# Unit 7 of the down projection as seven block products too, with some of the weight sums made by adding DMAs

## The reference

```python
h = rms_norm(x, ffn_norm[i])
u = causal_depthwise_conv(h @ w_up[i], conv_w[i], conv_b[i])
x = x + (jax.nn.silu(u[..., :D_FF]) * u[..., D_FF:]) @ w_down[i]
x = x + (p[i] @ ple_proj[i]) * jax.nn.sigmoid(x @ ple_gate[i])
```

## Time and profile before

| | us |
|---|---|
| median of 3 runs | 658.11 |
| lowest, highest | 657.94, 658.22 |
| profiled execution | 658.76 |
| its span in the trace | 656.9 |
| granted TensorE clock | 1.0 throughout |

### The profile page before, as it was taken

One profiled execution on the slowest core, in us unless ns is written; L12 is line 12 of the kernel. 1 busy time (PEld: TensorE's weight loads), 2 busy tenths in 40 slices (PEclk: granted clock), 3 DMA queues, 4 the chain that ended last, 5 costly groups with the idle time before them and its releaser, 6 DMA issues.

```text
span 656.9 us, 9644 instructions
## 1 busy us (share of the span) xinstructions
PE 648.3 (99%) x3774; PEld 558.8 (85%) x3774; DVE 507.4 (77%) x729; ACT 432.2 (66%) x649; POOL 329.4 (50%) x196
## 2 busy tenths in 40 slices
PE   8999999999999999999999999999999999999997
PEld 6988887888888888888889879878888888888885
DVE  5997778749878768996488777886699778789933
ACT  6669886676766674654474789856776766664632
POOL 5443500288888885006841353004888888820091
PEclk9999999999999999999999999999999999999999
DMA  9972125675555555653387431165555555555411
GB/s 320 372 252 65 65 101 160 198 247 192 189 187 191 185 189 191 212 196 108 109 287 248 154 102 65 66 196 189 193 192 193 191 189 189 188 194 204 161 32 65
DMA packets 74606, 115.38 MB, mean 176 GB/s; under 512 B 2368, under 2 KB 58432, under 8 KB 74304
## 3 DMA queue, kind: packets, MB, share of 16 engines
q1 hardware_dynamic: 73408, 111.95, 51.0%
q10 hardware_dynamic: 1152, 2.81, 1.2%
HBM read 113.70 MB, written 1.05 MB: 175 GB/s over the span
## 4 chain that ended last, share of the span: by engine, by line
PE 94%; DVE 3%; DMA 1%; ACT 1%; issue 0%; POOL 0%; SPq 0%; DVEq 0%; ACTq 0%; POOLq 0%
PE ps L1580 24%; PE ps L1027 14%; PE ps L1029 14%; PE ps L1028 14%; PE ps L1582 12%; PE ps L1173 1%; PE ps L1079 1%; DMA raw<-w_in 1%; PE ps L1199 1%; PE ps L1439 1%; PE ps L1041 1%; PE ps L1114 1%; PE ps L1211 1%; DVE hn L2286 1%; PE ps L1640 1%; PE ps L1642 1%
## 5 line engine op out<-in xcount | busy, mean ns | idle before, releaser
L496 POOL TENSOR_TENSOR wl<-raw,wh 128x2048 fp32r<-128x2048 f32 (+1 forms) x58 | 259.0, 4468 | 155.9 <-DVE x L2275 90.5
L1580 PE MATMUL ps<-hT_hl,wh 128*128 128x512 f32 x688 | 238.6, 392 | 0.0
L627 ACT ACTIVATE wh<-raw 128x2048 fp32r<-128x2048 f32 (+1 forms) x100 | 180.5, 1808 | 49.9 <-DVE raw L2216 23.6
L1582 PE MATMUL ps<-hT_hl,wl 128*128 128x256 f32 x688 | 193.3, 281 | 0.0
L1580 PEld LDWEIGHTS ps<-hT_hl,wh 128*128 128x128 f32 x688 | 129.1, 188 | 28.2
L1582 PEld LDWEIGHTS ps<-hT_hl,wl 128*128 128x128 f32 x688 | 129.4, 188 | 0.0
L1027 PE MATMUL ps<-wh,hT_hl 128*128 128x512 f32 (+1 forms) x216 | 79.7, 369 | 0.0
L1029 PE MATMUL ps<-wh,hT_hl 128*128 128x512 f32 (+1 forms) x216 | 77.4, 358 | 0.0
L1028 PE MATMUL ps<-wl,hT_hl 128*128 128x512 f32 (+1 forms) x216 | 77.4, 358 | 0.0
L483 POOL TENSOR_SCALAR st<-st 128x2 f32<-128x2 f32 (+3 forms) x22 | 6.5, 294 | 114.0 <-ACT lat L702 62.2
L2175 DVE SCALAR_TENSOR_TENSOR pb<-ps,conv,pb 128x255 f32<-128x255 f32 (+1 forms) x96 | 39.5, 472 | 17.3 <-ACT pb L918 17.3
(11 more groups left out here) (362 smaller groups left out, 1281.5 us busy)
## 6 DMA issues: line engine op xcount, KB each, us to landing
raw<-w_up SPq DMA_DIRECT2D x44, 1024.0 KB, 5.1
raw<-w_down SPq DMA_DIRECT2D x22, 1024.0 KB, 4.9
raw<-w_in SPq DMA_DIRECT2D x16, 1024.0 KB, 9.7
raw<-w_o SPq DMA_DIRECT2D x6, 1024.0 KB, 4.9
raw<-ple_gate SPq DMA_DIRECT2D x6, 1024.0 KB, 4.8
raw<-w_in SPq DMA_DIRECT2D x4, 704.0 KB, 5.2
ng<-norm_gains ACTq DMA_DIRECT2D x2, 1024.0 KB, 6.7
raw<-w_o SPq DMA_DIRECT2D x4, 512.0 KB, 4.0
```

The costliest lines, as they stand in the source:

```text
L496: pool.tensor_tensor(wl[:, slot, 0:n], raw[:, slot, 0:n], w_high(u)[:, 0:n].bitcast(F32), ALU.subtract).then_inc(done, 1)
L627: act.activation(w_high(u)[:, c:n], raw[:, slot, c:n], ACT.Copy).then_inc(h_made, 1)
L1580: pe.matmul(both, high[:, c], hU_all[:, k].rearrange("p a n -> p (a n)"), start=k == 0, stop=False, skip_group_check=True)
L1582: mm = pe.matmul(o, wl[:, slot, c], hU_h[:, k, :], start=False, stop=k == KT - 1, skip_group_check=True)
```

## The change

`SEVEN` gets unit 7, so that units 4, 6, 7 and 8 are made of seven products. The place for the sums is laid out anew: `t3` of all four units lies in the upper half of the region of `hT_hl`, t2 and t4 in two alternating places in the lower half.

Two of the four weight sums are now made by DMAs. When PE has finished the last up unit, SP copies the four b12 blocks (256 KB each) from w_down to their `t3` places, before it loads unit 5. POOL waits for all four, then adds b22 to `t3` of the first unit and b11 to b12 in the raw slot of the same unit with a DMA each, both ahead of its low part of down unit 2; those of the other three units are issued behind it, the second kind when the raw unit has landed. DVE adds only t2 and t4. ACT's high part of a seven unit waits for the DMA that makes the sum in the raw slot.

The sums of the activations (`act_sums`, unchanged) move from the down stage to the step of the up stage that follows the product, in the place where `product_low` stands for ordinary steps. `weight_rest` and the high parts of the weight sums become two instructions each.

```diff
@@ -75,7 +75,7 @@
-SEVEN = (4, 6, 8)
+SEVEN = (4, 6, 7, 8)
 FEW = len(SEVEN)
@@ -150,7 +150,8 @@
     "silu": STEPS, "prod": STEPS, "g_high": STEPS - FEW, "g_low": STEPS - FEW,
-    "w_sums": 4 * FEW, "a_sums": FEW, "a_rounded": FEW, "a_rest": FEW, "w_rounded": FEW, "w_rest": FEW,
+    "w_sums": 2 * FEW, "b12_landed": 16 * FEW, 
+    **{f"t{n}_made_{i}": 16 for n in (1, 3) for i in range(FEW)}, "a_sums": FEW, "a_rounded": FEW, "a_rest": FEW, "w_rounded": FEW, "w_rest": FEW,
     "down_low": STEPS - DVE_FROM, "sevens_done": 1, "sevens_copied": 2, "sevens_added": 1,
@@ -215,7 +216,7 @@
         hT = sb("hT", [P, KT, SEQ])
-        with nc.sbuf_tensor("quarters", [P, 2, 1536], F32) as quarters:
+        with nc.sbuf_tensor("quarters", [P, 4096], F32) as quarters:
             pass
@@ -319,9 +320,25 @@
+        def t3_sum(i):
+            return quarters[:, 2048 + i * 512:2048 + (i + 1) * 512]
+        def t3_low(i):
+            return hT_hl[:, 2048 + i * 512:2048 + (i + 1) * 512]
+        def t2_t4(i):
+            return quarters[:, (i % 2) * 1024:(i % 2 + 1) * 1024]
+        def weight_rows(i, k):
+            return slice((2 * SEVEN[i] + k) * P, (2 * SEVEN[i] + k + 1) * P)
...
-            return hT_hl[:, (i % 2) * 1536:(i % 2 + 1) * 1536]
+            return hT_hl[:, (i % 2) * 1024:(i % 2 + 1) * 1024]
@@ -438,6 +455,11 @@
                 for s in range(STEPS):
+                    if s == DEEP - 1:
+                        unit_done(sp, layer, U_DOWN - 1)
+                        for i in range(FEW):
+                            sp.dma_start(t3_sum(i), w_down[layer][weight_rows(i, 0), 0:512]
+                                         ).then_inc(F["b12_landed"], 16)
                     load(rows(w_down, 2 * s, 2), U_DOWN + s)
@@ -590,9 +612,31 @@
                 pool.wait_ge(F["hn_ready"], base["hn_ready"] + 4)
-                for u in (*range(U_POOL, U_DOWN + DVE_FROM), *range(U_GATE, UNITS)):
-                    if u == U_GATE:
-                        pool.wait_ge(F["sevens_added"], base["sevens_added"] + 1)
+                def add_to_t1(i):
+                    u = U_DOWN + SEVEN[i]
+                    slot = u % DEEP
+                    pool.wait_ge(raw_landed[slot],
+                                 (layer * (UNITS // DEEP) + u // DEEP + 1) * 16)
+                    pool.dma_start(raw[:, slot, 0:512], w_down[layer][weight_rows(i, 0), 512:1024],
+                                   accum_op=ALU.add).then_inc(F[f"t1_made_{i}"], 16)
+                def add_to_t3(i):
+                    pool.dma_start(t3_sum(i), w_down[layer][weight_rows(i, 1), 0:512],
+                                   accum_op=ALU.add).then_inc(F[f"t3_made_{i}"], 16)
+                for u in range(U_POOL, U_DOWN + DVE_FROM):
+                    if u == U_DOWN + DVE_FROM - 1:
+                        pool.wait_ge(F["b12_landed"], base["b12_landed"] + 16 * FEW)
+                        add_to_t3(0)
+                        add_to_t1(0)
+                    low(u)
+                for i in range(1, FEW):
+                    add_to_t3(i)
+                    add_to_t1(i)
+                pool.wait_ge(F["sevens_added"], base["sevens_added"] + 1)
+                for u in range(U_GATE, UNITS):
                     low(u)
@@ -944,8 +988,9 @@
                         act.wait_ge(F["g_low"], base["g_low"] + eights(STEPS - 1))
-                    act.wait_ge(F["w_sums"], base["w_sums"] + 4 * i + 4)
-                    act.activation(quarter_highs(i), quarters[:, i % 2], ACT.Copy
+                    act.wait_ge(F["w_sums"], base["w_sums"] + 2 * i + 2)
+                    act.activation(quarter_highs(i)[:, 0:1024], t2_t4(i), ACT.Copy)
+                    act.activation(quarter_highs(i)[:, 1024:1536], t3_sum(i), ACT.Copy
                                    ).then_inc(F["w_rounded"], 1)
@@ -967,7 +1012,7 @@
                     if s in SEVEN:
-                        act.wait_ge(F["w_sums"], base["w_sums"] + 4 * SEVEN.index(s) + 2)
+                        act.wait_ge(F[f"t1_made_{SEVEN.index(s)}"], 16 * (layer + 1))
                     high(U_DOWN + s)
@@ -1616,10 +1661,11 @@
                     product(6, s2, high, low, 0)
-                    mm = product(7, s3, high, low, 1)
+                    mm = split_product(ps[:, 7, :], *s3, high[:, 1024:1536], t3_low(i), i == 0,
+                                       i == FEW - 1)
                     if i == FEW - 1:
                         mm.then_inc(F["sevens_done"], 1)
-                    product(1, a22, high, low, 2).then_inc(w_used, 1)
+                    product(1, a22, high, low, 1).then_inc(w_used, 1)
@@ -2189,34 +2235,6 @@
-                dve.wait_ge(F["conv_landed"], base["conv_landed"] + 16)
-                for s in range(STEPS):
-                    summed(s, 0)
-                    if s and s - 1 not in SEVEN:
-                        product_low(s - 1)
-                    taps(s, 0)
-                    summed(s, 1)
-                    taps(s, 1)
-                    product(s)
-                product_low(STEPS - 1)
-                def weight_sums(i):
-                    u = U_DOWN + SEVEN[i]
-                    slot = u % DEEP
-                    dve.wait_ge(raw_landed[slot],
-                                (layer * (UNITS // DEEP) + u // DEEP + 1) * 16)
-                    unit_done(dve, layer, U_DOWN + SEVEN[i - 2] if i > 1 else U_DOWN - 1)
-                    b12, b11, b22, b21 = (raw[:, slot, n * 512:(n + 1) * 512] for n in range(4))
-                    t2, t3, t4 = (quarters[:, i % 2, n * 512:(n + 1) * 512]
-                                  for n in range(3))
-                    tt(t3, b12, b22, ALU.add).then_inc(F["w_sums"], 1)
-                    for n, (o, one, two) in enumerate(((b12, b12, b11), (t2, b12, b22),
-                                                       (t4, t2, b21))):
-                        tt(o, one, two, ALU.add).then_inc(F["w_sums"], 1)
-                        if n < 2:
-                            dve.wait_ge(F["w_sums"], base["w_sums"] + 4 * i + n + 2)
@@ -2229,6 +2247,32 @@
+                dve.wait_ge(F["conv_landed"], base["conv_landed"] + 16)
+                for s in range(STEPS):
+                    summed(s, 0)
+                    if s and s - 1 not in SEVEN:
+                        product_low(s - 1)
+                    elif s:
+                        act_sums(SEVEN.index(s - 1))
+                    taps(s, 0)
+                    summed(s, 1)
+                    taps(s, 1)
+                    product(s)
+                product_low(STEPS - 1)
+                def weight_sums(i):
+                    u = U_DOWN + SEVEN[i]
+                    slot = u % DEEP
+                    t2, t4 = (t2_t4(i)[:, n * 512:(n + 1) * 512] for n in range(2))
+                    dve.wait_ge(raw_landed[slot],
+                                (layer * (UNITS // DEEP) + u // DEEP + 1) * 16)
+                    unit_done(dve, layer, U_DOWN + SEVEN[i - 2] if i > 1 else U_DOWN - 1)
+                    dve.wait_ge(F[f"t3_made_{i}"], 16 * (layer + 1))
+                    tt(t2, t3_sum(i), raw[:, slot, 512:1024], ALU.add).then_inc(F["w_sums"], 1)
+                    dve.wait_ge(F["w_sums"], base["w_sums"] + 2 * i + 1)
+                    tt(t4, t2, raw[:, slot, 1536:2048], ALU.add).then_inc(F["w_sums"], 1)
@@ -2243,8 +2287,9 @@
                     dve.wait_ge(F["w_rounded"], base["w_rounded"] + i + 1)
-                    o = quarter_sums(i)
-                    tt(o, quarters[:, i % 2], quarter_highs(i).bitcast(F32), ALU.subtract
+                    highs = quarter_highs(i).bitcast(F32)
+                    tt(quarter_sums(i), t2_t4(i), highs[:, 0:1024], ALU.subtract)
+                    tt(t3_low(i), t3_sum(i), highs[:, 1024:1536], ALU.subtract
                        ).then_inc(F["w_rest"], 1)
@@ -2258,7 +2303,7 @@
                         weight_sums(SEVEN.index(s))
-                        act_sums(SEVEN.index(s))
+                        dve.wait_ge(F["w_sums"], base["w_sums"] + 2 * SEVEN.index(s) + 2)
                     down_low(s)
```

## The result

The changed kernel takes 664.35 us (median of 5 runs, 663.67 to 665.21), the kernel before 658.11 (657.89 to 658.28): a ratio of 1.0094, with an interval of 1.0083 to 1.0105. It is slower by 6.2 us. The forecast was 660.3, with a range of 656.6 to 664.0. The sign was right, the size was not: the loss is 4.1 us larger than forecast and ends just outside the range.

What follows compares the result with a forecast made beforehand. TensorE's matmul count plus PE's waits was taken as the bound. Per layer, 1.8 us of waits at units 2 and 8 less 0.68 saved, twice, adds 2.2 to 658.11: 660.3 us, range 656.6 to 664.0.

Steps and rivals of the forecast that it cites:

- The saving: Down stage, PE: unit 7 goes from 24 to 21 matmuls, 0.68 us a layer, 1.36 in all.
- The fourth sum: Up stage, step 9: VectorE's fourth activation sum starts 0.05 us after POOL's recorded start; taken to pass, at no cost.
- The gaps of 0.92, 0.79 and 0.66: Between POOL operations in up steps 5 and 7, 8, and 9; the fourth sum starts 0.71 us after POOL's end.
- a later sum of over 4 us: Sign of being wrong: any activation sum but the first of each four at over 4 us.
- Rival (1): Up step 9: fourth sum misses POOL's gap, waits 4.6 us; 3.5 - 0.68 = 2.8 a layer, 663.7; missed gap 15%.
- The landing at 253.4: Four b12 DMAs, 1024 KB together like one w_down load, start at 248.5 and land 4.9 us later.
- POOL's start of the issues at 253.5: Released by the copies, POOL issues two adding DMAs, starts unit 2's low part at 255.5, ends it at 260.1.
- Two branches, 1.8 each: Last up product held: PE waits 0.9 before unit 2, 0.9 before unit 8; product first: 1.8 before unit 2.
- The price of an issue: POOL's issue of an adding DMA: taken as 1.0 us, with bounds of 0.45 and 1.76.
- VectorE's chain of 26.24: From unit 3's low part to unit 8's activation rests VectorE needs 26.24 us, PE 25.16; a lead of 1.08 is needed.
- Landing of the adding DMAs "costs nothing": Sums by adding DMAs wanted after 263 for unit 4; landing can take 8 us, at no cost.

Runs made afterwards that it cites:

- With the gap mended: Changed kernel with only unit 8's activation sums moved out of step 9, behind the last low part of the up stage: 664.27 us, ratio 1.0090.
- the last kernel: Changed kernel with a semaphore for the first copy, unit 8's activation sums behind the last up low part, and its t2 made early: 657.80 us, ratio 0.9992.
- the kernel with t1 early: Changed kernel, unit 8's sums moved; POOL issues unit 4's t1 before unit 2's low part, waits for copies only behind it: 658.47 us, ratio 0.9998.

## Why the prediction was wrong

- *The saving* of 0.68 a layer, 1.36 in all, was right as far as the runs can tell: 1.07 by the medians, 1.24 by the means.
- *The fourth sum, "costed at nothing".* This is the step that failed first. The gaps of 0.92, 0.79 and 0.66 (measured 0.92, 0.80 and 0.66) and the start 0.05 behind POOL were right in both layers, and the text then set them aside on the ground that some time passes between a recorded start and the first read. The sum that started 0.05 behind was held for 4.72, so not even 0.05 of such time was there; the text had itself named a later sum of over 4 us as a sign of being wrong. Rival (1) describes what came and should have been the forecast: 3.5 of waits a layer (3.3 and 3.1 measured) and 663.7 (664.35 measured). Its parts were less exact than its sum. It has 1.4 before unit 1; measured were 0.94 before unit 0, where PE waits for VectorE's late taps, and 0.20 before unit 1. The half microsecond a layer of slower matmuls behind the gaps, on which the text had nothing, takes the total above 663.7.
- *The landing at 253.4, and POOL's start of the issues at 253.5.* This step failed too, and by itself it would have cost as much. The bytes were those of one load, and SP began to issue when it was expected to (248.47), but the fourth copy released POOL 6.0 later and not 4.9: at 254.3 to 254.6 in both layers of three kernels and one layer of a fourth, at 255.3 in its other layer, 0.8 to 1.8 later than the text has it (all with the last up matmul put at 248.24). With the gap mended the kernel still took 664.27, with 2.08 and 2.64 before unit 2 where the text has 0.9 or 1.8. Why four copies take longer than one load of the same bytes was not tried.
- *Two branches, 1.8 each.* The text had either a held product (0.9 before unit 2, 0.9 before unit 8) or a product that comes first and a late subtraction (1.8 before unit 2, nothing before unit 8). With the gap mended each branch occurs in one layer: the product is held in layer 0 (2.08 and 0.95) and takes 0.69 in layer 1, where its low part is held instead (2.64 and 0.45). They cost the same, as the text had it, but 3.03 and 3.09. The late landing explains most of the difference in both; unit 8's 0.45 in the second is the path named in the last point but one. That the two branches agreed was no check on the landing, which stands in both.
- *The price of an issue*, taken as 1.0, was right: from the start of the first issue (255.41) to the end of the subtraction (262.03) are 6.62, two issues of 1.0 and an operation of 4.62. The subtraction's record begins 0.6 before two issues of 1.0 would be over, and is 5.25 long, not 4.62.
- *VectorE's chain of 26.24.* Right to within 0.2: in the last kernel the low part of unit 3 ends at 263.0 and unit 8's remainders at 289.4. What the text missed beside it is the path from unit 6's end on PE to unit 8, 5.05 us beside the 4.76 of unit 7, which no lead at unit 3 shortens. In the kernel with t1 early it costs 0.45 a layer.
- *Landing of the adding DMAs "costs nothing".* Near enough in the changed kernel. They land after 7.3 and 8.0 in the median, where 8 were allowed, though single ones take up to 10.4; moved behind the low part they cost up to 1.2 us in all.

What stays open: whether the DMA share of about 1 costs anything by itself, which was not tested, and why the matmuls behind a gap are slower; the half microsecond a layer was read, not tried.

## What to carry to other kernels

Where an estimate puts a start within a few hundredths of the moment when another engine's operation would hold it, give the miss a large chance and its own price in the forecast. When two late things stand in one queue, taking one away may show nothing: undo each alone and both together before calling either harmless. A semaphore shared by four transfers is a wait for the last; where only the first is wanted next, give it one of its own (2.8 us here).

## What the runs showed of the hardware

- A VectorE instruction with both inputs in SBUF was held by a POOL tensor_tensor that stood only queued behind a DMA issue: 6.44, 6.25 and 6.23 us for a 128x512, begun 0.65, 0.45 and 0.44 before the subtraction's recorded start. Begun 1.19 before it, or inside an issue with a semaphore wait behind it, the same took 0.69. A 128x128 begun 0.05 behind a subtraction's recorded start took 4.72.
- POOL's issue of an adding DMA of 256 KB took 0.86 to 1.54 us in the changed kernel, 1.07 in the mean for t3 and 0.98 for t1; it landed 8.0 and 7.3 us later in the median, where a plain copy of the same size from SP took 3.7.
- The granted clock fell to 0.50, the level of 1.2 GHz, for some 3 us behind seven of the longer steps between two matmuls: 2.21 and 2.24 (unit 8's sums put back), 2.25 (the change without the fourth unit), 2.87 (unit 8's sums moved), 2.57, 2.80 and 4.03 (the fourth unit alone). It cost 1.6 us each where that was read, at 2.21, 2.24 and 2.87. It stayed at 1.00 behind steps of 2.08, 2.10, 2.17 and 2.31, behind a second one of 2.80, and behind the changed kernel's steps of 1.05 to 1.48. So the length of the step alone doesn't decide it in these traces; what does was not tried.
